# Attention probabilities scaled before they are turned, head outputs formed turned, and one branch's operand parts made earlier, in a fused two-block kernel

## The reference, cut to what matters

```python
o_a = swa_mixer(a_q, a_k, a_v, positions, swa_sinks[l])       # window of 128 keys, with a sink
o_b = nsa_mixer(b_q, ...)          # gate0 * o_cmp + gate1 * o_sel + gate2 * o_win
o_c = mla_mixer(c_qa, c_kv, c_kr, positions, ...)
g = sigmoid(g_br)
merged = (g[:, :, 0] * (o_a @ w_br_a[l])
          + g[:, :, 1] * (o_b @ w_br_b[l])
          + g[:, :, 2] * (o_c @ w_br_c[l]))
x = x + merged @ w_out[l]
```

## Time and profile before

| | |
|---|---|
| runs | 1672.26, 1678.62, 1679.55 us, median 1678.62 |
| the profiled execution | 1676.58 us, its span 1674.5 us |
| mean granted clock of TensorE | 0.986 of full speed |
| busy: PE, DVE, ACT, POOL | 95%, 56%, 39%, 2% of the span |
| the 18 steps of layer 0 and layer 1 | about 689 to 812 us and 1228 to 1351 us of the span |

### The profile page before, as it was taken

One profiled execution on the slowest core, in us unless ns is written; L12 is line 12 of the kernel. 1 busy time (PEld: TensorE's weight loads), 2 busy tenths in 40 slices (PEclk: granted clock), 3 DMA queues, 4 the chain that ended last, 5 costly groups with the idle time before them and its releaser, 6 DMA issues.

```text
span 1674.5 us, 22343 instructions
## 1 busy us (share of the span) xinstructions
PE 1594.9 (95%) x9359; PEld 1238.2 (74%) x9359; DVE 939.0 (56%) x1372; ACT 655.0 (39%) x962; POOL 27.2 (2%) x89
## 2 busy tenths in 40 slices
PE   5999999999999799999999999999999999999998
PEld 1998655454545377687788899878768888889986
DVE  3876676642222464566675665545466567556653
ACT  2543411111111243556545444335255744543441
POOL 1000010100000000000000000000000000000000
PEclk9999999999999999999999999999999999999999
DMA  8555519989999844332345365445424235435651
GB/s 307 188 189 201 201 53 333 385 328 414 390 423 380 335 144 144 86 142 108 129 155 183 117 197 174 183 160 185 154 76 151 101 127 192 158 130 186 201 181 71
DMA packets 153156, 333.36 MB, mean 199 GB/s; under 512 B 17763, under 2 KB 69221, under 8 KB 140773
## 3 DMA queue, kind: packets, MB, share of 16 engines
q1 hardware_dynamic: 147504, 326.94, 53.7%
q10 hardware_dynamic: 5558, 5.06, 0.9%
HBM read 330.94 MB, written 1.05 MB: 198 GB/s over the span
## 4 chain that ended last, share of the span: by engine, by line
PE 84%; DVE 8%; ACT 4%; DMA 2%; issue 1%; POOL 0%; ACTq 0%; POOLq 0%; DVEq 0%
PE ps_g L742 19%; PE ps_g L723 16%; PE ps_g L1148 7%; PE ps_g L1293 6%; PE ps_s L1549 4%; PE ps_p L1549 3%; PE ps_g L883 3%; PE ps_o L790 3%; PE ps_p L723 2%; DVE ring_r L2329 2%; PE ps_o L1177 2%; PE ps_x L1177 2%; PE ps_s L723 1%; PE ps_p L780 1%; PE ps_x L696 1%
## 5 line engine op out<-in xcount | busy, mean ns | idle before, releaser
L2329 DVE TENSOR_TENSOR ring_r<-ring,late_w 128x4096 fp32r<-128x4096 f32 (+1 forms) x50 | 217.0, 4339 | 153.3 <-ACT late_w L1887 153.3
L1887 ACT ACTIVATE late_w<-ring 128x4096 fp32r<-128x4096 f32 (+1 forms) x50 | 178.1, 3563 | 127.6 <-PE ps_p L1549 42.8
L742 PE MATMUL ps_g<-hf_high,ring_r 128*128 128x256 f32 x640 | 179.0, 280 | 0.0
L742 PE MATMUL ps_g<-hf_high,late_w 128*128 128x256 f32 x576 | 162.1, 281 | 0.0
L742 PE MATMUL ps_g<-h_t_r,late_w 128*128 128x256 f32 x576 | 161.2, 280 | 0.0
L742 PEld LDWEIGHTS ps_g<-hf_high,ring_r 128*128 128x128 f32 x640 | 122.0, 191 | 0.0
L742 PEld LDWEIGHTS ps_g<-h_t_r,late_w 128*128 128x128 f32 x576 | 108.6, 189 | 0.0
L742 PEld LDWEIGHTS ps_g<-hf_high,late_w 128*128 128x128 f32 x576 | 108.1, 188 | 0.0
L1911 ACT ACTIVATE arena<-arena,neg_max 128x256 f32<-128x256 f32 (+1 forms) x160 | 71.6, 451 | 39.4 <-DVE neg_max L2384 39.4
L1148 PE MATMUL ps_g<-arena 128*64 128x512 f32 x288 | 85.7, 599 | 0.0
L723 PE MATMUL ps_g<-early_w,first_low 128*128 128x512 f32 (+1 forms) x176 | 68.7, 390 | 3.9 <-ACT arena L1873 1.9
(11 more groups left out here) (704 smaller groups left out, 3714.3 us busy)
## 6 DMA issues: line engine op xcount, KB each, us to landing
ring<-in_w_in_dram SPq DMA_DIRECT2D x31, 2048.0 KB, 7.9
ring<-in_w_gate_up_dram SPq DMA_DIRECT2D x44, 1024.0 KB, 6.7
arena<-in_w_down_dram SPq DMA_DIRECT2D x16, 2048.0 KB, 13.9
ring<-in_w_mod_dram SPq DMA_DIRECT2D x10, 2048.0 KB, 11.1
ring<-in_w_down_dram SPq DMA_DIRECT2D x10, 2048.0 KB, 7.7
arena<-in_w_gate_dram SPq DMA_DIRECT2D x16, 1024.0 KB, 13.4
arena<-in_w_up_dram SPq DMA_DIRECT2D x8, 2048.0 KB, 16.0
ring<-in_w_gate_dram SPq DMA_DIRECT2D x8, 2048.0 KB, 14.5
```

The lines of the kernel that those rows point to most:

```text
L742: ins = pe.matmul(b.ap[:, (f % 2) * SEQ:(f % 2 + 1) * SEQ], a[:, k, f * P:(f + 1) * P], x[:, k, :], start=k == 0 and i == 0, stop=k == nk ...
L1887: act.activation(high_of(name, rnd)[:, 0:n], ring[:, slot, 0:n], ACT.Copy).then_inc(high_ready.sem, 1)
L2329: dve.tensor_tensor(ring_r[:, slot, 0:n], ring[:, slot, 0:n], high_of(name, rnd)[:, 0:n].bitcast(F32), ALU.subtract).then_inc(low_ready.se ...
```

## The change

For all steps but `cmp` the probabilities are divided by their sum before they are turned. A new `mixer_inverse(n)` on VectorE makes the reciprocal (times the branch gate), signals it, and multiplies heads 0 and 1 in place, one `tensor_scalar` each; GpSimd multiplies heads 2 and 3 in place in one `tensor_tensor`. TensorE's turn of n waits for both. `mixer_inverse(n + 1)` stands at the head of VectorE's iteration n, before the mask of n+2; inverse 0 stands behind the masks of 0 and 1. A `cmp` step is scaled by VectorE alone.

An output is formed turned: v is the stationary operand (128 keys x 64) and the turned probabilities are the moving one (128 queries), two heads of a pair into the two halves of the partitions. It is copied (or added) to `heads_t` as it is, and the 24 transposes are gone. The high and low parts of the outputs are made from `heads_t` in SBUF; those of o_a at steps 14 (ScalarE) and 15 (VectorE, in front of `make_low("bra")`) instead of after the steps, in places of their own. The diff, cut to its core:

```diff
 def mixer_turn(n):
-    turn_probs("layer", step, l)
+    pe.wait_ge(probs.sem, probs.at("layer", tag, l))
+    pe.wait_ge(probs_scaled, len(MIXER_STEPS) * l + n + 1)
+    pe.wait_ge(last_heads_scaled, len(WEIGHED) * l + WEIGHED.index(step) + 1)
+    claim(PT, tag, l)
+    for i in range(4):
+        for b in range(kbs):
+            ins = pe.transpose(p4[:, i, b, :], scores[:, n % 2, i, b * P:(b + 1) * P], ident[:, :])
+def turned_output(step, v):
+    claim(O, tag, l)
+    pe.wait_ge(PT.free, PT.nth("layer", tag, l))
+    for c in range(2):
+        for b in range(kbs):
+            for half in range(2):
+                ins = pe.matmul(O.ap[half * HD:(half + 1) * HD, c * P:(c + 1) * P], v(2 * c + half, b), probs_t[:, 2 * c + half, b, :],
+                                start=b == 0, stop=b == kbs - 1)
+    ins.then_inc(O.full, 1)
 # output of a cmp step
-pe.matmul(O.ap[:, :], probs_t[:, 0, 0, :], cmp_v..., start=True, stop=True)
+for c in range(KF):
+    ins = pe.matmul(O.ap[:, c * P:(c + 1) * P], v[:, c * P:(c + 1) * P], probs_t[:, 0, 0, :], start=True, stop=True)
...
-for name, src in (("a", o_a), ("b", o_b), ("c", o_c)):
-    ...
-    turn_rows(f"o{name}", [lambda tb, k=k, s=src: s[:, tb, k * P:(k + 1) * P] for k in range(KF)], l)
...
 # TensorE, before the branch products
-for name in "ab":
-    turned("layer", f"o{name}", 2, l)
+for i, name in enumerate("ab"):
+    pe.wait_ge(heads_low_ready, 6 * l + 2 * i + 2)
     product_wide("layer", f"br{name}", (o_high[name], o_low[name]), l)
...
 # GpSimd, before the root of "mem"
+for n, step in enumerate(MIXER_STEPS):
+    if step[0] != "cmp":
+        pool.wait_ge(inverse_ready, len(WEIGHED) * l + WEIGHED.index(step) + 1)
+        p = scores[:, n % 2, 2:4, 0:keys_of(step)]
+        pool.tensor_tensor(p, p, rden[:, n % 2, 2:4].unsqueeze(2).broadcast_to([P, 2, keys_of(step)]), ALU.mult)\
+            .then_inc(last_heads_scaled, 1)
...
 # ScalarE
+def heads_high(name):
+    act.wait_ge(O.free, O.nth("layer", step_tag(last), l))
+    for r in range(2):
+        act.activation(o_high[name][:, 2 * r:2 * r + 2, :], heads_t[name][:, 2 * r:2 * r + 2, :], ACT.Copy).then_inc(x_high.sem, 1)
 for n, step in enumerate(MIXER_STEPS):
     if n + 1 < len(MIXER_STEPS):
         mixer_exp(n + 1)
+    if n == FIRST_MLA:
+        heads_high("a")
...
-for name in "abc":
-    turned_high(f"o{name}", KF, o_high[name], l)
+for name in "bc":
+    heads_high(name)
...
 # VectorE
+def mixer_inverse(n):
+    ...
+    st.done(dve.reciprocal(inv, total))
+    st.settle()
+    ...
+    dve.sem_inc(inverse_ready, 1)
+    for i in range(2):
+        p = scores[:, n % 2, i, 0:keys_of(step)]
+        ins = dve.tensor_scalar(p, p, rden[:, n % 2, i:i + 1], None, ALU.mult)
+    ins.then_inc(probs_scaled, 1)
...
+    if step[0] == "win":
+        dve.tensor_tensor(out_t, out_t, sums, ALU.add).then_inc(O.free, 1)
     else:
+        dve.tensor_copy(out_t, sums).then_inc(O.free, 1)
...
+def heads_low(name):
+    for r in range(2):
+        dve.wait_ge(x_high.sem, x_high.at("layer", f"o{name}{r}", l))
+        dve.tensor_tensor(o_low[name][:, 2 * r:2 * r + 2, :], heads_t[name][:, 2 * r:2 * r + 2, :],
+                          o_high[name][:, 2 * r:2 * r + 2, :].bitcast(F32), ALU.subtract).then_inc(heads_low_ready, 1)
 mixer_mask(0)
 mixer_mask(1)
+mixer_inverse(0)
 for n, step in enumerate(MIXER_STEPS):
-    if step[0] == "cmp":
-        total_blocks(n, step)
+    if n + 1 < len(MIXER_STEPS):
+        mixer_inverse(n + 1)
     if n + 2 < len(MIXER_STEPS):
         mixer_mask(n + 2)
     mixer_finish(n)
...
     if n == FIRST_MLA + 1:
+        heads_low("a")
         make_low("bra", rnd=l)
-for name in "abc":
-    turned_low(f"o{name}", KF, o_low[name], o_high[name], l)
+for name in "bc":
+    heads_low(name)
 make_low("brb", rnd=l)
```

More of the change, by code:

```diff
@@ L464, in two_blocks @@
         cmp_blk = arena[:, at + 2112:at + 3136].rearrange("p (v j n) -> p v j n", v=2, j=16)
-        cmp_tmp = arena[:, at + 3136:at + 3136 + HALF].rearrange("p (h d) -> p h d", d=HD)
-        o_a, o_b, o_c = (view(at + 1024 * i, TB, HALF) for i in range(3))
+        o_a = view(at, TB, HALF)
+        heads_t = {name: view(at + 1024 * i, KF, SEQ) for i, name in enumerate("abc")}
         lat_t = view(at + 1024, 5, SEQ)
@@ L626, in two_blocks @@
         rows = Named(sem("rows_ready"), first=(1, ["h_left", "h_right", "gy0", "gy1", "mg0", "mg1", "h2_0", "h2_1"]),
-                     layer=(LAYERS, ["swa", "nsa", "twice", "lat", "mk", "blk", "hcv", "mla_v", "ob", "mem", "merged"]))
+                     layer=(LAYERS, ["swa", "nsa", "twice", "lat", "mk", "blk", "hcv", "mla_v", "mem", "merged"]))
         masked = Named(sem("scores_masked"), first=(1, [step_tag(s) for s in FOX_STEPS]), layer=(LAYERS, [step_tag(s) for s in LAYER_STEPS]))
@@ L632, in two_blocks @@
         g_col_ready, last_used = sem("g_col_ready"), sem("last_used")
+        probs_scaled, heads_low_ready = sem("probs_scaled"), sem("heads_low_ready")
+        inverse_ready, last_heads_scaled = sem("inverse_ready"), sem("last_heads_scaled")
+        WEIGHED = [step for step in MIXER_STEPS if step[0] != "cmp"]
         bg_tanhed, cmp_tanhed = sem("bg_tanhed"), sem("cmp_tanhed")
@@ L1384, in _ @@
                     mixer_output(n)
-                for name, src in (("a", o_a), ("b", o_b), ("c", o_c)):
-                    if name == "b":
-                        pe.wait_ge(rows.sem, rows.at("layer", "ob", l))
-                    else:
-                        pe.wait_ge(O.free, O.nth("layer", step_tag((SWA_STEPS if name == "a" else MLA_STEPS)[-1]), l))
-                    turn_rows(f"o{name}", [lambda tb, k=k, s=src: s[:, tb, k * P:(k + 1) * P] for k in range(KF)], l)
                 def mem_half(r):
@@ L1408, in _ @@
                 mem_half(0)
-                turned("layer", "oc", 2, l)
+                pe.wait_ge(heads_low_ready, 6 * l + 6)
                 w = split_chunk("brc", KF, D, l)
@@ L2195, in mixer_exp @@
                     act.activation(scores[:, n % 2, 0, 0:P], scores[:, n % 2, 0, 0:P], ACT.Exp, scale=-1.0).then_inc(probs.sem, 1)
+                def heads_high(name):
+                    last = {"a": SWA_STEPS, "b": WIN_STEPS, "c": MLA_STEPS}[name][-1]
+                    act.wait_ge(O.free, O.nth("layer", step_tag(last), l))
+                    for r in range(2):
+                        act.activation(o_high[name][:, 2 * r:2 * r + 2, :], heads_t[name][:, 2 * r:2 * r + 2, :], ACT.Copy).then_inc(x_high.sem, 1)
                 mixer_exp(0)
@@ L3203, in total_blocks, with block_of @@
                     st.settle()
+                    dve.tensor_tensor(block_scores(n), block_scores(n), over(rden[:, n % 2, :], CMP), ALU.mult).then_inc(probs_scaled, 1)
+                def block_of(step, chunks):
+                    return heads_t["b" if step[0] in ("sel", "cmp", "win") else "a" if step[0] == "swa" else "c"][:, chunks, step[2] * P:(step[2] + 1) * P]
                 def finish_blocks(n, step):
-                    tag, o = step_tag(step), o_b[:, step[2], :].rearrange("p (h d) -> p h d", d=HD)
+                    tag, o = step_tag(step), block_of(step, slice(0, KF))
+                    dve.wait_ge(O.free, O.nth("layer", step_tag(MIXER_STEPS[n - 1]), l))
@@ L3208, in finish_blocks @@
                     dve.wait_ge(O.full, O.nth("layer", tag, l))
-                    dve.tensor_tensor(cmp_tmp, O.ap[:, :].rearrange("p (h d) -> p h d", d=HD), over(rden[:, n % 2, :], HD), ALU.mult).then_inc(O.free, 1)
+                    dve.tensor_tensor(o, o, O.ap[:, :].rearrange("p (c q) -> p c q", q=P), ALU.add).then_inc(O.free, 1)
                     dve.wait_ge(O.free, O.nth("layer", tag, l))
-                    st.done(dve.tensor_tensor(o, o, cmp_tmp, ALU.add))
-                    st.settle()
+                def mixer_inverse(n):
+                    step = MIXER_STEPS[n]
+                    if step[0] == "cmp":
+                        total_blocks(n, step)
+                        return
+                    total, inv = den[:, n % 4, 0:4], rden[:, n % 2, 0:4]
+                    dve.wait_ge(probs.sem, probs.at("layer", step_tag(step), l))
+                    if step[0] == "swa":
+                        st.done(dve.tensor_tensor(total, total, sink_e[:, n % 4, 4:8], ALU.add))
+                        st.settle()
+                    st.done(dve.reciprocal(inv, total))
+                    st.settle()
+                    if step[0] in ("sel", "win"):
+                        inv4 = inv.rearrange("p (f r) -> p f r", f=2)
+                        st.done(dve.tensor_tensor(inv4, inv4, branch(1 + (step[0] == "win"), step), ALU.mult))
+                        st.settle()
+                    dve.sem_inc(inverse_ready, 1)
[3 more added lines that the diff above has]
+                    ins.then_inc(probs_scaled, 1)
```

39 lines of the change are left out of this document (18 added, 21 removed).

## The result

The changed kernel took 1688.15 us (median of 5 runs, 1683.52 to 1694.22) beside 1677.52 for the kernel before: ratio 1.0073, 95% interval 1.0043 to 1.0103. It is slower by 10.6 us by the medians and by 12 by the means, which the ratio compares; 1673 was predicted. The profiled execution is the fastest of the five: 1683.52 us, span 1681.5, mean clock 0.982. The other four had mean clocks of 0.977 to 0.979.

The account below looks back on a forecast made before the run. TensorE's own queue was taken to bound the kernel, 84% of the span being its work. Gains of 2.2 us in layer 0 and 3.4 in layer 1, together 5.6 off the 1678.6 median, gave 1673 us, range 1665 to 1683.

Parts of the forecast that it names:

- Outputs formed turned: TensorE's outputs in steps 3 to 13: 1.2 and 0.65 us each, saving 2.9 us a layer (0 to 5.1).
- All that PE gained by then is lost and some more: -0.6: Start of the steps: VectorE's scaling and blocks delay turns 0 and 2 and scores 4, losing 0.6 us (0 to 1.5).
- One before and one after: Clock at the start of the steps: one low stretch before the change and one after it, so no time charged.
- Middle stalls +1.0: Middle steps: TensorE's stalls of 0.8 and 0.6 us shrink because VectorE finishes cmp steps faster, gaining 1.0 (0 to 1.4).
- the scaling of middle steps is hidden: Middle two-block steps: 7.1 us of work from turn n fits within about 9.5 until turn n+2, so no wait.
- Turn 17: End of the steps: VectorE's 4.4-us low part delays this turn, a new 5.3-us stall that nearly cancels 5.5 us removed.
- GpSimd's multiplication: Scaling of heads 2 and 3 on GpSimd: 1.1 us for a two-block step, 0.6 for a one-block step.
- rival 3: GpSimd's multiplication is long, 3.5 us an operation, so turns wait: 18 us slower, 1697; chance 0.12.
- Rival 2: VectorE's and GpSimd's scalings hold each other up, 2.9 us a layer, eating the gain: no change, 1679; chance 0.22.
- a clock that stays low: Another way to Rival 2's time: the clock stays low as long as in the earlier trace's second window, -3.5.

Follow-up runs that it names:

- e13: The changed kernel timed and profiled again without any edit: 1692.8 us, ratio 1.0092 to the kernel before.
- e9: The changed kernel with the compressed blocks made by GpSimd instead of VectorE: 1681.7 us, ratio 1.0021 to the kernel before.
- e14: The changed kernel once more without any edit, one run only: 1691.7 us.
- e1: The changed kernel with the first branch's low weights on VectorE moved behind inverse 17 and finish 16: 1680.0 us, ratio 1.0014 to the kernel before.
- e3: The changed kernel with VectorE scaling all four heads and GpSimd left out: 1688.6 us, ratio 1.0075 to the kernel before.
- e12: The changed kernel with the first branch's high and low output parts made behind the steps again: 1694.1 us, ratio 1.0091 to the kernel before.
- e4: The changed kernel without scaling the probabilities except in cmp steps, for timing only (result lacks the division): 1668.1 us, ratio 0.9951 to the kernel before.
- e16: As e11, but with GpSimd scaling heads 2 and 3 again: 1666.7 us, ratio 0.9951 to the kernel before.
- e11: Changed kernel with blocks on GpSimd, first-branch low weights behind inverse 17, step 0's second gate part before turn 0, VectorE scaling all heads: 1664.6 us, ratio 0.9912.
- e15: The kernel before with compressed blocks made by GpSimd and step 0's second gate part in front of turn 0: 1680.8 us, ratio 1.0034.

## Why the prediction was wrong

It forecast 1673, with 0.15 for slower; 1688 was measured. In the two mixers 4.7 us were to be gained; the first profile lost 2.4 there and the more usual e13 14.8. Nearly all of the 12.4 us between these two is clock. By its own steps:

- **Outputs formed turned: right.** 1.03 and 0.58 us an output where 1.2 and 0.65 were taken. From turn 5 to turn 6 the step is 0.56 shorter (6.63 and 6.07 us), 0.53 predicted; from turn 4 to turn 5 0.11 (5.30 and 5.19), 0.2 predicted; four of each make 2.7 for the 2.9. A pair of 128 columns at the full rate would have given 0.86 and 0.43.
- **"All that PE gained by then is lost and some more: -0.6": mis-sized, 2.4.** Turn 0 came 2.9 us later against scores 1 (2.5 predicted), but then turn 2 1.8 and scores 4 2.4. VectorE's 4.5 us of blocks ended at 1250.8, in old times 1243.8 where 1242 to 1243 was expected, and inverse 2 (1.4 us with its scaling) and mask 3 both stand behind them. The order had been named; that the path now runs through VectorE's sum from mask 1 to mask 3, with every new operation in it, had not been added up. The lock was in this too: VectorE's pair of multiplications was costed by the earlier trace rows at about 0.6 and 0.5 us a step and took 1.44 and 0.88. e9 shows the cause: with the blocks gone these waits are gone.
- **"One before and one after": the step that failed most.** The clock at the start was costed at no change, because a stretch at half clock stood there before as well. But there are now two waits where there was one, 2.8 and then 1.3 to 1.5 us, and the term measured 0 only in the first profile. In e13 and e14 half clock for 10 to 11 us follows the second wait. Up to turn 3 e13 is 6.2 and 4.8 us longer than the first profile, 11.0 of the 14.8 us by which its two mixers exceed those of the kernel before. e1, e3's layer 1, e12 and e4 have the like. The second window of the earlier trace rows could have warned, but was read too simply. TensorE is busy for 7.62 of its 14 us, by its rows about 6 of them at half clock, so some 3 of the 5.2 us called lost fall on work and the rest on standing still. What it shows is two waits, one close behind the other, and a clock that is still low about 4 us behind the second:

```profile
581.07 1.12 PE L1225 MATMUL ps_x<-ident,x_rows 128*128 128x128 f32 x4 [4.81 <-DVE x_rows L3027]
...
586.35 0.55 PE L1248 MATMUL ps_s<-early_w,first_low 128*128 128x256 f32 x1 [3.31 <-DVE h_t_r L2317]
```

- **Middle stalls +1.0: wrong.** The wait for the mask fell from 0.56 to 0.24, the 0.82 for the gate bank stayed, and the query transposes before step 14 wait 0.91 where it was 0.29, so nothing is gained. That the scaling of middle steps is hidden came true, although the cover was added up too short: two steps of 11.9 us less 1.0 and the 0.7 of the outputs leave 10.2, not 9.5.
- **Turn 17: right.** 5.38 us of stall for 5.3, behind the 4.4-us low part as described, though what ends last is VectorE's scaling and not GpSimd's; from there to the branch 6.3 for 6.6 with the clock. The two waits of outputs 15 and 16 for ScalarE's copies, 1.6 us, were not foreseen; they lie within the stall. From turn 14 to turn 17 it is 0.9 more than predicted.
- **GpSimd's multiplication: right**, 1.04 and 0.61 us for 1.1 and 0.6, so rival 3 was ruled out.
- **Rival 2** had the right mechanisms and too small a sum. The lock is real: e3, e9 and e16 show it. The Trainium skill states it ("SBUF — State Buffer", Who interferes with whom), and these runs agree: GpSimd's operation beside it makes VectorE's pair 1.44 us, where four alone take 1.14. But in e11's mixers it costs 1.2 us a layer, not 2.9. Its alternative, a clock that stays low, is the larger term. I treated them as different ways to no change; they come together, and with the start that makes slower.

What the working could have told: each of its two exposed ends was costed as a delay of one turn, and the clock as one stretch for one wait. The waits were counted by their length, not by what the clock does behind each.

Open: what decides whether the long low stretch follows. The wait before turn 2 was 1.12, 1.21 and 1.30 us in the three mixers without it and 1.41 to 2.40 in the nine with it, but no run sets this wait by itself, and the half clock behind turn 0 differs among them too. A wait alone doesn't bring it: 1.68 us before output 0 in e15 and 1.2 before turn 0 in e11 were followed by full clock.

## What to carry to other kernels

When operations are added in front of a step that another engine waits for, add up that engine's whole queue from the last point where it was ahead, and ask which operation can leave the engine, before trying orders: three orders at the start only moved the wait, and the move off VectorE took it away and let the filler pay. (Where an order puts a 4.4-us operation behind what is waited for and nothing else comes late, as in e1, it pays by itself.) A new wait of one or two microseconds on TensorE can cost five more in clock, and one profile need not show it: look at the mean clock of all runs before trusting the stages of one. Work split over VectorE and GpSimd at the same moment was slower here than on VectorE alone. GpSimd paid with a whole piece, the blocks, though even that held VectorE's rotation up; a place where VectorE is idle was not tried.

## What was not expected of the hardware

- Two VectorE multiplications beside one of GpSimd took 1.44 us, four without it 1.14; a run of eight VectorE operations beside GpSimd's took 3.44 for 1.24.
- The same kernel had a granted clock of 1.00 or of 0.68 to 0.72 over the 16 to 18 us around turn 3, worth 5 us a layer; in e1 it was 0.53 over 14 us in which TensorE was busy throughout.
- Parts of the kernel that no edit touched varied by 5 us (the first 685 us) and 4 us (between the mixers) from profile to profile, and by 3.2 and 2.6 in three of the same kernel.
- Three waits of TensorE of 1.2 to 1.7 us had different sequels: full clock in e15 and e11, half clock for 3.7 us behind 1.49 us in the kernel before.
